# Seven block products for the gate chunks of the conv branch in a two-layer streaming encoder

## The chip, the cores and the metric

One core of a Trainium2 chip runs the whole program as one launch. The metric is the device time of the run in microseconds. A core has a matrix engine (TensorE, PE in the profile), VectorE (DVE), ScalarE (ACT), GpSimd (POOL) and SyncE (SP), each with a queue of its own that runs in order, and semaphores between them.

## What is computed

The reference is one step of a two-layer encoder on 544 token columns (512 of a prompt and 32 of a running stream) with 1024 channels. In each layer three branches, each 512 wide, are merged by sigmoid gates:

```python
gates = jax.nn.sigmoid(g.reshape(bsz, t_len, N_BRANCH, D_MODEL) + b_gate)
merged = (gates[:, :, 0] * (y_a @ w_branch[0])
          + gates[:, :, 1] * (y_b @ w_branch[1])
          + gates[:, :, 2] * (y_c @ w_branch[2]))
x = layer_norm(DN_ALPHA * x + merged @ w_out, ln1_g, ln1_b)
```

`g` is a slice of `x @ w_in`, so each branch's gate is a 1024 by 1024 matrix on the token columns. `y_a` comes from a width-31 convolution followed by a layer norm and SiLU, `y_b` from a gated mixing over 128 rows, `y_c` from stick-breaking attention. A ConvGLU channel mixer (w_up, a width-3 convolution, w_down) follows.

## The kernel before

**Numbers in two parts.** Every float32 operand of a matmul is split into a rounded high part (fp32r) and the rest: ScalarE writes the high part by a copy, VectorE the low part by a subtraction. A product is then three matmuls of 128 by 128 weights on 272 columns, high·high, high·low, low·high (`three_of`, lines 2053 to 2061).

**Tiles.** The 544 columns are two halves of 272 (`HALF`). Weights come in chunks: 2048 columns hold 8 contraction tiles of 256 outputs. A chunk gives four *units*, two output tiles times two halves, each in a PSUM bank `ps[0..3]` (named `acc`); unit b has output tile b % 2 and half b // 2. A unit over 8 contraction tiles is 24 matmuls, over 4 tiles 12.

**The ring of weights.** SP loads chunks in a fixed order into three slots (`raw`, `wh`, `wl`; `SLOT`, line 67), and waits for a slot until TensorE's first matmul after the slot's last use. The fourth w_out chunk (`OUT_LAST`) has a slot of its own in space of the convolution. ScalarE's `hi()` (line 577) and VectorE's `lo()` (line 1186) split the chunks in the same order.

**The branches.** Each layer takes them in the order attention, mixing, convolution (n = 0, 1, 2), each as four pairs i = 0..3 of a gate chunk (4 units of 24 matmuls) and a branch chunk (4 units of 12). The third branch's pairs are lines 2372 to 2374 on TensorE. ScalarE's `gates` (line 854) turns the four gate banks into sigmoids in `tmp`; VectorE's `products` (line 1587) multiplies them with the branch banks and adds to `merged` (lines 1608, 1611); for n = 2 ScalarE copies `merged` to `mh` (line 882), VectorE writes `ml` (line 1597), and both feed w_out. The order of each queue is written out by hand: in pair 0 of the third branch VectorE runs `lo()`, `conv_lo` (8 instructions at line 1225, the low part `yal` of `y_a`), `lo()`, `products(0, 2)`; ScalarE runs `conv_write` (lines 891, 893), then `gates(0, 2)`, then the `mh` copies.

**Seven products elsewhere.** In the FFN, 19 of the 22 pairs of w_up chunks already multiply a 2 by 2 block matrix with seven products instead of eight (`products` on TensorE, line 2412; sums of weights on VectorE, lines 1846 to 1866; sums of tokens T1 to T4N, line 1791). There the sums of a quad are made one to two quads ahead.

**POOL** is little used: masks for attention and, per layer, the low part of one w_up chunk (line 561).

Of the kernel before, what the change touches and what calls it, by code (L numbers as in the profile page):

```python
# [5 lines left out]
F32 = mybir.dt.float32  # L6
F32R = mybir.dt.float32r
# [4 lines left out]
P = 128  # L12
# [131 lines left out]
def trunk(nc, adds, x_in, win, wbr, wout, wup, wdn, par_in, bc_in, sguw_in, kc_in, vc_in, gh_in, fh_in,  # L144
          y_out, k_out, v_out, glu_out, ffn_out, sgu_out):
    with ExitStack() as ctx:
        sems = {}

        def sem(name):
            sems[name] = ctx.enter_context(nc.semaphore(name))  # L150
            return sems[name]
# [41 lines left out]
        mv = sb("mv", [P, 5, 2])  # L193
        rs = sb("rs", [P, 2, 5])

        gex = sb("gex", [P, 2, GEX])
        C = top[0]
        cbuf = sb("cbuf", [P, 2, GEX - 2])
# [55 lines left out]
        sqc = [sb("sqc0", [P, CT, HALF], at=F + 90016), sb("sqc1", [P, CT, HALF], at=F + 71168)]  # L254

        cst = [st0[:, :], cbuf[:, 0, 0:HALF]]
        csd = [st1[:, :], cbuf[:, 0, HALF:2 * HALF]]
# [96 lines left out]
        back_hi = sem("back_hi")  # L354
        fst_made = sem("fst_made")
        s_ready = sem("s_ready")
        prod_full = sem("prod_full")
        snapped = sem("snapped")
        combined = sem("combined")
# [34 lines left out]

        def dve_at(l, what, q):
            return l * len(DVE_ORDER) + DVE_PLACE[what, q]

        def first_chunk(l):
            return l * LAYER + 45
# [8 lines left out]
        def _(sp):  # L408
# [29 lines left out]
            for l in range(DEPTH):  # L438
# [81 lines left out]
        def _(pool):  # L520
# [18 lines left out]
            for r in range(DEPTH):  # L539
                pool.wait_ge(late_full, c.take(late_full, 64))  # L540
                g.affine_select(out=wsgu[:, :, :], in_=wsgu[:, :, :], compare_op=ALU.is_ge, fill=0.0, base=0,
                                         pattern=[[0, CT], [1, P]], channel_multiplier=-1).then_inc(
                                             sgu_masked, c.up(sgu_masked))

                for n in range(STEPS):
                    w = (n % 4 + 1) * P
                    for b in range(2):
                        pool.wait_ge(sig_full[b], c.take(sig_full[b]))
                        for t, fill in ((keep[b][:, T - P:T], 1.0), (beta[n % 2][b][:, w - P:w], 0.0)):
                            g.affine_select(out=t, in_=t, compare_op=ALU.is_gt, fill=fill, base=0, pattern=[[-1, P]],  # L550
                                            channel_multiplier=1).then_inc(mask_full[b], c.up(mask_full[b]))
                for b in range(2):
                    c.skip(sig_full[b], 2)

                j = r * LAYER + POOL_LO
# [16 lines left out]
        def _(act):  # L572
# [161 lines left out]
            for l in range(DEPTH):  # L734
# [119 lines left out]
                def gates(i, n, after=None, first=None):  # L854
# [50 lines left out]
                for n in range(3):  # L905
                    for i in range(4):
# [3 lines left out]
                            act.wait_ge(sgu_stored, c.take(sgu_stored, 16))  # L910
                        if n == 1 and i == 3:
                            gates(i, n, first=lambda: [conv_root(h) for h in range(2)])
                        else:
                            gates(i, n, mixed_hi if (n, i) == (0, 3) else squares if (n, i) == (1, 2) else None)
# [38 lines left out]
                      ACT.Copy).then_inc(fst_made, 1)  # L953

                def conv_taps(i):
                    act.wait_ge(acc_free[3], c.seen(acc_free[3]))
                    act.wait_ge(gex_full, c.take(gex_full))
                    for m in range(2):
# [182 lines left out]
        def _(dve):  # L1141
# [269 lines left out]
            for l in range(DEPTH):  # L1411
# [169 lines left out]
                def gated_lo():  # L1581
                    for g_ in range(CT):
                        dve.wait_ge(yb_hi, c.take(yb_hi))
                        v.tensor_tensor(yb[1][:, g_, :], gv[:, g_, :], yb[0][:, g_, :].bitcast(F32),
                                                 ALU.subtract).then_inc(yb_full, c.up(yb_full))

                def products(i, n):

                    for b in range(4):
# [303 lines left out]
                def gated_values(q):  # L1893
# [3 lines left out]
                    if q + 1 < QUADS:  # L1897
# [136 lines left out]
        def _(pe):  # L2034
# [199 lines left out]
            for r in range(DEPTH):  # L2234
# [342 lines left out]
```

## Time and profile before

| | us |
|---|---|
| runs: 1743.92, 1744.11, 1744.28; median | 1744.11 |
| profiled execution, its own time | 1744.08 |
| its span, first to last instruction | 1742.3 |
| TensorE busy | 1729.0 |
| VectorE busy | 1347.0 |
| ScalarE busy | 856.4 |
| POOL busy | 101.2 |

The span is what the timeline shows; the 1.8 us around it belong to the run's time. A matmul's listed length is its way through the pipeline, and matmuls overlap: what one costs is the distance from start to start. The same holds, less strongly, for VectorE and ScalarE, whose next instruction may start shortly before the last one ends. The third branch of layer 0 lies at 373 to 445 us, that of layer 1 at 1234 to 1306 us.

### The profile page before, as it was taken

The page shows a single profiled execution, that of the slowest core. Times are in us where ns is not written, and L with a number is a line of the kernel's source. Part 1 is how long each engine was busy: PE and PEld are TensorE (multiplying, and loading weights), DVE is VectorE, ACT ScalarE, POOL GpSimd, SP SyncE. Part 2 cuts the span into 40 slices and gives each one's busy share as a digit, 9 for nine tenths or more (in the row PEclk, how much of TensorE's full clock was granted, in tenths as well). Part 3 has the DMA queues.
Part 4 walks back from the last instruction along what each step waited for, and adds up shares of the span by engine and source line. Part 5 has one row for each costly group of instructions (what it writes and reads, how often), then busy time and mean ns, then how long its engine had stood idle before and what let it go on. Part 6 is the DMA issues. An engine that isn't in the chain of part 4 may idle for free.

```text
span 1742.3 us, 32677 instructions
## 1 busy us (share of the span) xinstructions
PE 1729.0 (99%) x13778; PEld 1694.6 (97%) x13778; DVE 1347.0 (77%) x1927; ACT 856.4 (49%) x1400; POOL 101.2 (6%) x159
## 2 busy tenths in 40 slices
PE   9999999999999999999999999999999999999997
PEld 9998899999999999999999989999999999999997
DVE  5698778664689999876667887777557999998675
ACT  4246532263366655644452565333534656656443
POOL 0025100000010000000000350000001000000000
PEclk9999999999999999999999999999999999999999
DMA  5432122222223223355524221222232222223544
GB/s 177 152 121 74 37 92 81 73 86 97 77 72 120 98 97 100 107 181 177 168 98 155 94 74 62 75 85 90 81 98 97 74 98 97 97 100 132 177 164 135
DMA packets 36513, 185.99 MB, mean 107 GB/s; under 512 B 7376, under 2 KB 11728, under 8 KB 18192
## 3 DMA queue, kind: packets, MB, share of 16 engines
q1 hardware_dynamic: 34672, 176.28, 30.3%
q10 hardware_dynamic: 1696, 7.64, 1.3%
q8 instruction: 109, 1.79, 0.4%
q14 instruction: 36, 0.29, 0.1%
HBM read 176.75 MB, written 7.15 MB: 106 GB/s over the span
## 4 chain that ended last, share of the span: by engine, by line
PE 96%; DVE 3%; issue 1%; DMA 0%; ACT 0%; ACTq 0%; DVEq 0%
PE acc L2055 23%; PE acc L2061 22%; PE acc L2060 22%; PE score L2055 5%; PE score L2061 5%; PE score L2060 5%; PE small L2060 1%; PE small L2061 1%; PE small L2055 1%; PE score L2131 1%; PE turned L2060 1%; PE turned L2061 1%; PE turned L2055 1%; PE small L2182 1%; PE turned L2162 1%; DVE acc L1397 1%
## 5 line engine op out<-in xcount | busy, mean ns | idle before, releaser
L2055 PE MATMUL acc<-xh,wh 128*128 128x272 f32 x1880 | 551.2, 293 | 1.3 <-DVE xl L1147 1.2
L2061 PE MATMUL acc<-xh,wl 128*128 128x272 f32 x1880 | 541.7, 288 | 0.0
L2060 PE MATMUL acc<-xl,wh 128*128 128x272 f32 x1880 | 541.1, 288 | 0.0
L1193 DVE TENSOR_TENSOR wl<-raw,wh 128x2048 fp32r<-128x2048 f32 (+2 forms) x116 | 231.5, 1995 | 171.5 <-ACT wh L584 170.9
L2055 PEld LDWEIGHTS acc<-xh,wh 128*128 128x128 f32 x1880 | 354.1, 188 | 8.8 <-issue 5.0
L2060 PEld LDWEIGHTS acc<-xl,wh 128*128 128x128 f32 x1880 | 354.2, 188 | 0.1
L2061 PEld LDWEIGHTS acc<-xh,wl 128*128 128x128 f32 x1880 | 353.2, 188 | 0.0
L584 ACT ACTIVATE wh<-raw 128x2048 fp32r<-128x2048 f32 (+2 forms) x136 | 232.7, 1711 | 162.7 <-DMA raw<-wdn 115.0
L2055 PE MATMUL acc<-fhh,wh 128*128 128x272 f32 x704 | 204.2, 290 | 0.1
L2060 PE MATMUL acc<-fll,wh 128*128 128x272 f32 x704 | 202.5, 288 | 0.0
L2061 PE MATMUL acc<-fhh,wl 128*128 128x272 f32 x704 | 202.4, 288 | 0.0
L1397 DVE SCALAR_TENSOR_TENSOR acc<-glu,par,acc 128x574 f32<-128x574 f32 x240 | 181.1, 812 | 0.1
L862 ACT ACTIVATE tmp<-acc,par 128x272 f32<-128x272 f32 x96 | 46.6, 488 | 195.5 <-PE acc L2061 195.2
L2055 PEld LDWEIGHTS acc<-fhh,wh 128*128 128x128 f32 x704 | 132.6, 188 | 0.7 <-issue 0.5
L2060 PEld LDWEIGHTS acc<-fll,wh 128*128 128x128 f32 x704 | 132.4, 188 | 0.2
L2061 PEld LDWEIGHTS acc<-fhh,wl 128*128 128x128 f32 x704 | 132.4, 188 | 0.0
L2055 PE MATMUL score<-th,shi 128*128 128x272 f32 x304 | 88.4, 291 | 0.0
L2061 PE MATMUL score<-th,slo 128*128 128x272 f32 x304 | 87.8, 289 | 0.0
L2060 PE MATMUL score<-tl,shi 128*128 128x272 f32 x304 | 87.1, 287 | 0.0
L2055 PE MATMUL acc<-mh,wh 128*128 128x272 f32 x256 | 74.9, 293 | 0.0
L2060 PE MATMUL acc<-ml,wh 128*128 128x272 f32 x256 | 73.8, 288 | 0.0
L2061 PE MATMUL acc<-mh,wl 128*128 128x272 f32 x256 | 73.7, 288 | 0.0
(325 smaller groups left out, 3939.5 us busy)
## 6 DMA issues: line engine op xcount, KB each, us to landing
raw<-win SPq DMA_DIRECT2D x50, 1024.0 KB, 5.0
raw<-wup SPq DMA_DIRECT2D x44, 1024.0 KB, 5.0
raw<-wdn SPq DMA_DIRECT2D x32, 1024.0 KB, 4.9
raw<-wbr SPq DMA_DIRECT2D x24, 512.0 KB, 3.6
raw<-wdn SPq DMA_DIRECT2D x16, 768.0 KB, 4.2
raw<-wout SPq DMA_DIRECT2D x8, 1024.0 KB, 4.9
v_out<-vfm ACTq DMA_DIRECT2D x2, 1088.0 KB, 9.2
k_out<-k ACTq DMA_DIRECT2D x2, 1088.0 KB, 4.9
```

What stands on the lines that cost most here:

```text
L584: A(wh[s][:, 0:n], raw[s][:, 0:n], ACT.Copy).then_inc(hi_full[s], c.up(hi_full[s]))
L862: A(tmp[:, b, :], ps[b][:, 0:HALF], ACT.Sigmoid, bias=col(par, PAR["b_gate"] + 8 * BRANCHES[n] + 2 * i + b % 2)).then_inc(acc_free[b], c.u ...
L1193: v.tensor_tensor(wl[s][:, 0:n], raw[s][:, 0:n], wh[s][:, 0:n].bitcast(F32), ALU.subtract).then_inc(lo_full[s], c.up(lo_full[s]))
L1397: v.scalar_tensor_tensor(out=acc[:, m, :], in0=glu_at(m, j), scalar=w, in1=acc[:, m, :], op0=ALU.mult, op1=ALU.add).then_inc(vec, c.up(vec))
L2055: first = mm(out, a, xs[0], start=start, stop=False, skip_group_check=onto)
L2060: mm(out, a, xs[1], start=False, stop=False, skip_group_check=onto)
L2061: return mm(out, b, xs[0], start=False, stop=stop, skip_group_check=onto)
L2131: last = mm(bs[b][:, 0:w], yc[x][rows, ht, i * P:w], ks[y][rows, ht, 0:w], start=x + y == 0, stop=y == 1)
L2162: last = pe.transpose(bt[:, kb * P:(kb + 1) * P], beta[n % 2][part][:, kb * P:(kb + 1) * P], ident[:, :])
L2182: last = mm(bo[DH * b:DH * b + DH, kb * P:SEQ], vtok[:, kb, h * DH:(h + 1) * DH], blocks.rearrange("p a n -> p (a n)"), start=kb == 0, sto ...
```

## The change

In the third branch, the gate chunks of pairs 1 to 3 are computed as block products with seven multiplications; pair 0 stays as it was. The chunk's 2 by 2 blocks are A11, A12 (contraction tiles 0 to 3 and 4 to 7 of output tile 0) and A21, A22 (of output tile 1). The tokens are halved in the same way. Each product is 4 tiles times 3 matmuls = 12 matmuls, 84 in all against 96:

| | product | bank |
|---|---|---|
| 1 | A11 · x(0..3, half 0) | GA = `bs[0]`, then snapshot m1 |
| 2 | A12 · x(4..7, half 0) | GB = `bo` |
| 3 | (A21 + A22 − A11) · T2 | on top of GA, then snapshot u1 |
| 4 | (A11 − A21) · T3 | GC = `bs[1]` |
| 5 | (A21 + A22) · T1 | on top of GA, then snapshot u3 |
| 6 | (A12 − (A21 + A22 − A11)) · x(4..7, half 1) | on top of GA |
| 7 | A22 · T4N | on top of GC |

The gates are: unit 0 from GB + m1, unit 3 from GC + u3 (before product 7), unit 2 from GA after product 6, unit 1 from GC + u1 after product 7. TensorE runs products 1 to 5, branch unit 0, product 6, branch unit 1, product 7, branch units 2 and 3.

- **POOL** makes the four token sums T1, T3, T2, T4N once per layer, 1088 columns each, in buffers of the convolution, after the variance matmuls of the convolution's layer norm.
- **ScalarE** splits them in pair 0, between its gates, after waiting for the end of `conv_lo`; it also splits the weights and weight sums and takes the snapshots.
- **VectorE** makes the weight sums (four of 512 columns per pair), their low parts, the low parts of the token sums, and the three additions of snapshots per pair. In pair 0 these preparations of pair 1 stand ahead of `products(0, 2)`.
- **SP** waits for product 5 of pair 3 before it loads the fourth w_out chunk, whose slot lies in the same buffers.
- The squares of the convolution's norm (`sqc`) move to other space; two columns of `gex` are zeroed again by VectorE.

The diff, cut to what orders the work:

```diff
@@ sync
                     if i == 3:
                         sp.wait_ge(ya_full, c.take(ya_full, 2 * CT))
+                        sp.wait_ge(gprod_full, 7 * gquad(l, 3) + 5)
@@ gpsimd
+                pool.wait_ge(glu_stored, 16 * 2 * CT * (r + 1))
+                pool.wait_ge(ln_var, 2 * (r + 1))
...
+                    if n > 1:
+                        pool.wait_ge(gt_made, 4 * r + (1 if n == 2 else 3))
+                    g.tensor_tensor(gtraw[j][:, :, :], a, b, ALU.subtract).then_inc(gt_made, 1)
@@ scalar, gates(i, n)
-                        if n == 2 and b == 2:
-                            hi()
+                def gate_turned_hi(j):
+                    act.wait_ge(gt_made, 4 * (l + 1))
+                    act.wait_ge(ya_full, 2 * CT * (l + 1))
+                    A(gth[j][:, :, :], gtraw[j][:, :, :], ACT.Copy).then_inc(gt_hi, 1)
+                def make_ready(b):
+                    if b == 0:
+                        gate_turned_hi(T2)
+                        gate_turned_hi(T3)
+                    if b == 1:
+                        gate_turned_hi(T1)
+                        gate_turned_hi(T4N)
+                    if b == 2:
+                        gate_first_blocks(1)
+                        gate_second_blocks(1)
+                    if b == 3:
+                        gate_two_sums(1)
+                        gate_last_sum(1)
+                def block_gates(i):
+                    gate_snapshot("m1", i, 1)
+                    hi()
+                    gate_snapshot("u1", i, 3)
+                    gate_sigmoid(i, 0, 1)
+                    gate_snapshot("u3", i, 5)
+                    gate_sigmoid(i, 3, 2)
+                    if i == 3:
+                        hi()
+                    gate_first_blocks(i + 1)
+                    gate_two_sums(i + 1)
+                    gate_sigmoid(i, 2)
+                    gate_last_sum(i + 1)
+                    gate_second_blocks(i + 1)
+                    gate_sigmoid(i, 1, 3)
...
+                        elif n == 2 and i:
+                            block_gates(i)
@@ vector, block_products(i)
+                    gate_add(i, 0, GB, "m1", 2, 1)
+                    lo()
+                    gate_add(i, 3, GC, "u3", 5, 3)
+                    gate_three_sums(i + 1)
+                    if i == 3:
+                        lo()
+                    one(0)
+                    gate_fourth_sum(i + 1)
+                    gate_first_low(i + 1)
+                    gate_two_lows(i + 1)
+                    gate_add(i, 1, GC, "u1", 7, 2)
+                    one(1)
+                    if i == 3:
+                        low(0)
+                        low(1)
+                    gate_back_low(i + 1)
+                    one(2)
+                    one(3)
...
                 for h in range(2):
                     conv_lo(h)
-                lo()
+                gate_turned_lo(T2)
+                gate_turned_lo(T3)
+                gate_three_sums(1)
+                gate_fourth_sum(1)
+                gate_turned_lo(T1)
+                gate_first_low(1)
+                gate_back_low(1)
+                gate_two_lows(1)
+                gate_last_low(1)
                 products(0, 2)
-                for i in range(3):
-                    lo()
-                    lo()
-                    products(i + 1, 2)
+                gate_turned_lo(T4N)
+                for i in range(1, 4):
+                    block_products(i)
...
+                v.memset(gex[:, :, 0:2], 0.0).then_inc(gex_zeroed, 1)
                 history(0)
@@ tensor
-                for i in range(4):
-                    chunk()
-                    chunk(xs=ya, nk=CT, first=ya_tiles if i == 0 else None)
+                chunk()
+                chunk(xs=ya, nk=CT, first=ya_tiles)
...
+                    if p == 2:
+                        pe.wait_ge(lo_full[s], c.take(lo_full[s]))
+                    if i > 1 and p in (1, 2, 4):
+                        pe.wait_ge(*{1: (gate_made, 4 * q - 1), 2: (gcombined, 3 * q - 2), 4: (gcombined, 3 * q)}[p])
+                    if p in (3, 5, 6):
+                        pe.wait_ge(gsnapped, 3 * q + {3: 1, 5: 2, 6: 3}[p])
+                    if p in (3, 6):
+                        pe.wait_ge(gs_ready, 2 * q + {3: 1, 6: 2}[p])
+                    if p == 7:
+                        pe.wait_ge(gcombined, 3 * q + 2)
+                    turned = {3: T2, 4: T3, 5: T1, 7: T4N}.get(p)
+                    if i == 1 and turned is not None:
+                        pe.wait_ge(gt_ready, 4 * r + G_ORDER[turned])
...
+                for i in range(1, 4):
+                    s = arrived()
+                    for p in range(1, 6):
+                        gate_product(i, p, s)
+                    sb_ = arrived()
+                    unit(sb_, 0, 0, ya, CT)
+                    gate_product(i, 6, s)
+                    unit(sb_, 1, 1, ya, CT)
+                    gate_product(i, 7, s)
+                    unit(sb_, 2, 0, ya, CT)
+                    unit(sb_, 3, 1, ya, CT, done=True)
```

`gate_snapshot` copies bank GA to an SBUF buffer; `gate_sigmoid` waits for its addition or product and writes `tmp`; `gate_add` adds a bank and a snapshot; `one(b)` is the two product instructions of unit b, `low(b)` the `ml` instruction. The four `mh` copies of a pair stay in ScalarE's `products(i, 2)`, which runs after `gates` or `block_gates` of that pair and before those of the next.

## Rows read from the trace of the kernel before

**Rows 1.** the page, part 1: busy us (share of the span), instructions

```profile
PE 1729.0 (99%) x13778; PEld 1694.6 (97%) x13778; DVE 1347.0 (77%) x1927; ACT 856.4 (49%) x1400; POOL 101.2 (6%) x159
```

**Rows 2.** TensorE's waits, whole run: waited for, us in total, times, longest

```profile
PE acc L2055 <- DVE xl L1147: 1.2, 1, 1.2
```

**Rows 3.** TensorE's timeline: start us, us, instruction; first matmuls of three stages

```profile
385.16 0.29 PE L2055 MATMUL acc<-yah,wh 128*128 128x272 f32 x1
...
391.20 0.29 PE L2055 MATMUL acc<-xh,wh 128*128 128x272 f32 x1
...
403.23 0.29 PE L2055 MATMUL acc<-yah,wh 128*128 128x272 f32 x1
```

**Rows 4.** busy time by window: us, then PE, PEld, DVE, ACT, POOL

```profile
391.00:409.00 18.00, 18.00 (x145) 18.00 (x145) 8.44 (x15) 6.43 (x10) 0.00 (x0) 1.00 0.28 88
```

**Rows 5.** ScalarE's timeline, 350 to 420 us

```profile
354.80 0.49 ACT L594 ACTIVATE st<-small,eps 128x272 f32<-128x272 f32 x1 [0.31 <-PE small L2110]
...
381.37 1.48 ACT L862 ACTIVATE tmp<-acc,par 128x272 f32<-128x272 f32 x3
```

**Rows 6.** POOL's timeline, 1340 to 1355 us

```profile
1345.54 5.63 POOL L561 TENSOR_TENSOR wl<-raw,wh 128x512 fp32r<-128x512 f32 x4 [296.62 <-ACT wh L584]
```

**Rows 7.** VectorE's timeline, 350 to 420 us and 1346 us

```profile
368.86 0.44 DVE L1608 TENSOR_TENSOR tmp<-acc,tmp 128x272 f32<-128x272 f32 x1 [5.93 <-PE acc L2061]
...
369.70 2.28 DVE L1193 TENSOR_TENSOR wl<-raw,wh 128x2048 fp32r<-128x2048 f32 x1
...
381.23 2.90 DVE L1225 TENSOR_TENSOR yal<-acc,yah 128x272 fp32r<-128x272 f32 x8
...
386.93 0.44 DVE L1608 TENSOR_TENSOR tmp<-acc,tmp 128x272 f32<-128x272 f32 x1
...
388.44 0.44 DVE L1608 TENSOR_TENSOR tmp<-acc,tmp 128x272 f32<-128x272 f32 x1 [0.59 <-PE acc L2061]
...
391.47 0.44 DVE L1608 TENSOR_TENSOR tmp<-acc,tmp 128x272 f32<-128x272 f32 x1 [0.35 <-PE acc L2061]
...
392.31 1.02 DVE L1597 TENSOR_TENSOR ml<-merged,mh 128x272 fp32r<-128x272 f32 x2
...
1346.09 1.42 DVE L1234 TENSOR_TENSOR st<-cbuf 128x272 f32<-128x272 f32 x1
```

**Rows 8.** ScalarE's groups, shapes apart: busy us, mean ns of one | idle before

```profile
L981 ACT ACTIVATE wh<-raw 128x1024 fp32r<-128x1024 f32 x38 | 40.4, 1062 | 59.0 <-DVE raw L1852 59.0
...
L1002 ACT ACTIVATE m<-score 128x272 f32<-128x272 f32 x38 | 15.0, 395 | 11.5 <-PE score L2061 10.9
...
L882 ACT ACTIVATE mh<-merged 128x272 fp32r<-128x272 f32 x32 | 13.8, 431 | 42.3 <-DVE merged L1611 42.3
...
L968 ACT ACTIVATE th<-traw 128x1088 fp32r<-128x1088 f32 x8 | 8.9, 1112 | 3.7 <-DVE traw L1791 3.6
```

**Rows 9.** VectorE's groups, shapes apart, the same columns

```profile
L1816 DVE TENSOR_TENSOR wl<-raw,wh 128x1024 fp32r<-128x1024 f32 x38 | 46.3, 1218 | 0.0
...
L1846 DVE TENSOR_TENSOR sraw<-raw 128x512 f32<-128x512 f32 x38 | 26.0, 684 | 1.2 <-DMA raw<-wup 1.2
...
L1797 DVE TENSOR_TENSOR tl<-traw,th 128x1088 fp32r<-128x1088 f32 x8 | 10.1, 1286 | 0.1
```

**Rows 10.** VectorE's timeline in the FFN, 559 to 562 us

```profile
559.23 1.22 DVE L1808 TENSOR_TENSOR wl<-raw,wh 128x1024 fp32r<-128x1024 f32 x1
560.36 1.22 DVE L1816 TENSOR_TENSOR wl<-raw,wh 128x1024 fp32r<-128x1024 f32 x1
```

**Rows 11.** timelines of VectorE and ScalarE, 446 to 455 us

```profile
448.92 2.29 DVE L1193 TENSOR_TENSOR wl<-raw,wh 128x2048 fp32r<-128x2048 f32 x1 [1.37 <-ACT wh L584]
...
450.55 1.92 ACT L584 ACTIVATE wh<-raw 128x2048 fp32r<-128x2048 f32 x1 [1.67 <-DMA raw<-wout]
```

**Rows 12.** busy time and granted clock by window at the end: columns as above, PEclk after POOL

```profile
1731.00:1734.00 3.00, 0.93 (x4) 0.42 (x3) 2.54 (x4) 1.21 (x3) 2.50 (x3) 1.00 0.00 0
1734.00:1737.00 3.00, 0.00 (x0) 0.00 (x0) 2.93 (x4) 0.93 (x2) 1.43 (x2) 0.56 0.00 0
```

More of the change, by code:

```diff
@@ L356, in trunk @@
         s_ready = sem("s_ready")
+        gt_made = sem("gt_made")
+        gt_hi = sem("gt_hi")
+        gt_ready = sem("gt_ready")
+        gs_made = sem("gs_made")
+        gs_hi = sem("gs_hi")
+        gs_ready = sem("gs_ready")
+        gback_hi = sem("gback_hi")
+        gprod_full = sem("gprod_full")
+        gsnapped = sem("gsnapped")
+        gcombined = sem("gcombined")
+        gate_made = sem("gate_made")
+        gex_zeroed = sem("gex_zeroed")
         prod_full = sem("prod_full")
@@ new lines, in gate_fourth_sum, with gate_first_low @@
+                def gate_fourth_sum(i):
+                    if i < 4:
+                        a11, a12, a21, a22 = gate_blocks(i)
+                        q = gquad(l, i)
+                        dve.wait_ge(gs_made, 4 * q + 3)
+                        if i > 1:
+                            dve.wait_ge(gprod_full, 7 * (q - 1) + 6)
+                        v.tensor_tensor(gate_sum(2), a12, gate_sum(1), ALU.subtract).then_inc(gs_made, 1)
+                def gate_first_low(i):
+                    if i < 4:
+                        s, n = SLOT[turn[0]], CHUNK // 2
+                        assert turn[0] == gate_chunk(l, i)
+                        turn[0] += 1
+                        dve.wait_ge(hi_full[s], c.take(hi_full[s]))
+                        dve.wait_ge(gs_made, 4 * gquad(l, i) + 3)
+                        v.tensor_tensor(wl[s][:, 0:n], raw[s][:, 0:n], wh[s][:, 0:n].bitcast(F32), ALU.subtract).then_inc(
+                            lo_full[s], c.up(lo_full[s]))
@@ new lines, in gate_last_low, with gate_add @@
+                def gate_last_low(i):
+                    if i < 4:
+                        dve.wait_ge(gs_hi, 2 * gquad(l, i) + 2)
+                        v.tensor_tensor(gslo4[:, :], gsraw4[:, :], gshi4[:, :].bitcast(F32), ALU.subtract).then_inc(
+                            gs_ready, 1)
+                def gate_add(i, b, bank, name, product, snapshot):
+                    dve.wait_ge(gprod_full, 7 * gquad(l, i) + product)
+                    dve.wait_ge(gsnapped, 3 * gquad(l, i) + snapshot)
+                    dve.wait_ge(m_sum, c.seen(m_sum) if b != 1 else c.seen(m_sum, 1))
+                    v.tensor_tensor(tmp[:, b, :], bank[:, 0:HALF], snap[0][name][:, :], ALU.add).then_inc(gcombined, 1)
@@ new lines, in block_products, with one, low @@
+                def block_products(i):
+                    def one(b):
+                        t, cols = 2 * i + b % 2, (b // 2 * HALF, (b // 2 + 1) * HALF)
+                        dve.wait_ge(gate_made, 4 * gquad(l, i) + (1, 4, 3, 2)[b])
+                        dve.wait_ge(acc_full[b], c.take(acc_full[b]))
+                        v.tensor_tensor(tmp[:, b, :], ps[b][:, 0:HALF], tmp[:, b, :], ALU.mult).then_inc(
+                            acc_free[b], c.up(acc_free[b]))
+                        dve.wait_ge(acc_free[b], c.seen(acc_free[b]))
+                        v.tensor_tensor(row(merged, t, *cols), row(merged, t, *cols), tmp[:, b, :], ALU.add).then_inc(
+                            m_sum, c.up(m_sum))
+                    def low(b):
+                        t, cols = 2 * i + b % 2, (b // 2 * HALF, (b // 2 + 1) * HALF)
+                        dve.wait_ge(m_hi, c.take(m_hi))
+                        v.tensor_tensor(row(ml, t, *cols), row(merged, t, *cols), row(mh, t, *cols).bitcast(F32),
+                                        ALU.subtract).then_inc(m_ready[b // 2], c.up(m_ready[b // 2]))
+                    gate_add(i, 0, GB, "m1", 2, 1)
[16 more added lines that the diff above has]
+                    one(3)
+                    if i < 3:
+                        low(0)
+                        low(1)
+                    gate_last_low(i + 1)
+                    low(2)
+                    low(3)
@@ L2371, in ya_tiles, with gate_product @@
                         pe.wait_ge(ya_full, c.take(ya_full))
-                for i in range(4):
-                    chunk()
-                    chunk(xs=ya, nk=CT, first=ya_tiles if i == 0 else None)
+                chunk()
+                chunk(xs=ya, nk=CT, first=ya_tiles)
+                pe.wait_ge(mixed_used, c.seen(mixed_used))
+                def gate_product(i, p, s):
+                    q = gquad(r, i)
+                    if p == 2:
[11 more added lines that the diff above has]
+                        pe.wait_ge(gt_ready, 4 * r + G_ORDER[turned])
+                    bank = {2: GB, 4: GC, 7: GC}.get(p, GA)
+                    for t in range(4):
+                        if p in (1, 2, 4, 7):
+                            at = {1: t * 256, 2: (4 + t) * 256, 4: t * 256 + P, 7: (4 + t) * 256 + P}[p]
+                            w = [x[s][:, at:at + P] for x in (wh, wl)]
+                        elif p == 6:
+                            w = [x[:, t * P:(t + 1) * P] for x in (gshi4, gslo4)]
+                        else:
+                            w = [x[:, {5: 0, 3: 1}[p], t * P:(t + 1) * P] for x in (gshi, gslo)]
+                        if turned is None:
+                            tile, h = {1: (t, 0), 2: (4 + t, 0), 6: (4 + t, 1)}[p]
+                            mv_ = [x[:, tile, dcol(h)] for x in xs]
+                        else:
+                            mv_ = [x[turned][:, t, :] for x in (gth, gtl)]
+                        last = three_of(bank[:, 0:HALF], w, mv_, p in (1, 2, 4) and t == 0, t == 3, p not in (1, 2, 4))
+                    last.then_inc(gprod_full, 1)
+                    if p == 7:
+                        read.append(s)
```

93 lines of the change are left out of this document (91 added, 2 removed).

## The prediction, on record before the kernel ran

> **What bounds the kernel now.** I read the page's busy shares first. TensorE is busy for 99% of the span, VectorE for 77%, ScalarE for 49% [rows 1]. Next I read TensorE's waits over the whole run: the longest single one is 1.2 us, at the very start [rows 2]. So every matmul that goes away saves its own time, and every wait put on TensorE's queue costs its full length; nothing later can take up either. The price of a matmul comes from TensorE's timeline in the third branch: the branch half of pair 0 starts at 385.16, that of pair 1 at 403.23, one pair of 144 matmuls apart, so 18.07/144 = 0.1255 us each, and a unit of 12 costs 1.51 us [rows 3]. The listed 0.29 us of a matmul is its length in the pipeline, not its price. Last I looked at what the other two engines have to do in one such pair: VectorE 8.44 us, ScalarE 6.43 us of 18 [rows 4]. They look idle, but they run strictly in order, and their order is what the change rewrites. I therefore worked along their queues.
>
> All times below are those of layer 0. Layer 1 has the same program, so per-layer figures are doubled.
>
> **What goes away.** Each of three pairs per layer needs 84 gate matmuls in place of 96: 36 per layer, 72 in all, 72 × 0.1255 = 9.04 us [rows 3].
>
> **POOL's four sums.** They wait for the variance matmuls, whose result ScalarE reads at 354.80 [rows 5]. POOL's 512-column subtractions took 5.63 us for four, 2.75 ns a column, so 1088 columns cost 3.0 us and four sums 12 us: done by about 367 [rows 6]. The first reader is ScalarE after 381.85 [rows 5]. Behind POOL's new wait stands only its later split of one w_up chunk. VectorE can suffer: a 272-column addition of two SBUF operands took 1.42 us beside POOL, where 272-column instructions otherwise take 0.44 [rows 6, 7]. The bounds are no delay, and 12 us of VectorE held, of which 5.93 us is its idle time before 368.86 [rows 7]. The remaining 6.1 us would move the split of gate chunk 0 from 369.70 to 375.8, its end to 378, and TensorE, which is due to start on it at 373.1, would be 5 us late. I book nothing for it, since that loss would fall inside the larger wait worked out next, which begins from ScalarE's work and not from TensorE's. The Trainium skill, "SBUF — State Buffer", says of the engine ports that VectorE and GpSimd take their shared pair as an exclusive lock for a whole instruction when a VectorE instruction has two SBUF inputs. By that rule the four 3.0 us sums would hold VectorE one after another, which is the upper bound above; the 1.42 us row agrees, and the sum stays the same.
>
> **The first block pair (the term that decides).** ScalarE's split of the token sum T2 waits until VectorE has finished all of `yal`, at 381.23 + 2.90 = 384.13 [rows 7]. Queued behind that wait on ScalarE stand three of pair 0's four gates and all preparations of pair 1. With 1.11 us for T2 [rows 8], VectorE may start T2's low part at 385.30. From there its queue holds, before the products of pair 0: three 1088-column lows, four 512-column sums, three 1024-column lows, one 512-column low. Their durations are 1.29, 0.68 and 1.22 us [rows 9]; back to back an instruction starts 0.09 before its forerunner ends (559.23 + 1.22 against 560.36) [rows 10]. Two sums wait for the one before, 0.12 each. So 3 × 1.20 + 4 × 0.60 + 0.24 + 3 × 1.13 + 0.60 = 10.2 us, and the first product starts at 395.5. (ScalarE's twelve pieces in the same stretch come to some 9 us, so it does not set this.) In the trace of before, the products of pair 0 stand at 386.93, and their second pair of lows starts at 392.31, 5.38 us later, with 0.59 and 0.35 us of waiting for TensorE in it: 4.44 us of work [rows 7]. The last sum is then ready at about 400.0. ScalarE still has to copy it to `mh` (0.43) and only then, in its order, comes snapshot m1 of pair 1 (0.40) [rows 8]: 400.9 with hand-overs.
>
> TensorE's side: pair 1 starts at 391.20 if nothing waits, and product 3 of it, two units later, at 394.21 [rows 3]. Product 3 writes into the bank that m1 is read from, and waits for the snapshot. **So 400.9 − 394.2 = 6.7 us per layer are lost there.** About 1.9 us of it shows earlier, since the gates of units 2 and 3 of pair 0, pushed behind the token splits, hold their banks until 389.1 (384.16, four splits of 1.02, gate 1, gate 2) and 391.6 (two 1024-column splits of 0.97 and gate 3 more), where the branch units want them at 388.2 and, after that delay, 390.7 [rows 3, 5, 8]; the other 4.6 to 4.8 us is one wait at product 3. The bounds: 5.5 us if hand-overs are free and ScalarE gets in earlier, 8 us if issue gaps come in.
>
> **The pairs after it.** From the end of product 7 the chain is: addition, gate 1, two product instructions, a 1024-column low, four more product instructions, `mh`, m1. With the durations above that is 5.9 to 6.1 us, against four units = 6.03 us until product 3 of the next pair. I take 0.15 us for each of two hand-overs, 0.3 per layer (bounds 0 and 0.8). The work itself fits: VectorE gains about 5 us per pair (three additions, four sums, one and a half lows), 13.7 of 16.6; ScalarE about 2.4.
>
> **The second w_out chunk.** Its ring slot was freed six units before the stage's end. Now it is freed after product 7, two units before it (−3.0). The third chunk shows the latency: slot free at 391.20 + 3 × 18.07 = 445.4, split begun at 450.55 when the transfer let go [rows 11]. So +5.1, then 1.92 and 2.29 for the two splits [rows 11]: ready at +6.4 against +6.0, where TensorE has used up the first chunk. Before, it was ready at 451.2 against 451.4. I take 0.4 us per layer (bounds 0 and 1).
>
> **At no cost.** SP's new wait before the fourth w_out chunk is over nine units before that chunk's turn, hidden by the third chunk's wait for its slot; uncovered, it would hold the w_up loads behind it. The two zeroed columns of `gex` are one small VectorE instruction ahead of a much longer ScalarE chain; if that cover went it would be some 0.2 us.
>
> **The sum.** Profiled execution 1744.08 (its span of 1742.3 and 1.8 around it; the median of the runs is 1744.11, so nothing to convert). 1744.08 − 9.04 + 2 × (6.7 + 0.3 + 0.4) = **1749.8 us**. The change takes 9 us of matmuls away and gives 14.8 back as waits, nearly all of it where the stage goes over to the block products.
>
> **Rivals.**
> *A. TensorE alone decides (faster).* If the snapshot m1 of pair 1 came before 394.2, with pair 1's preparations fitting beside pair 0, only the w_out wait stays: 1744.08 − 9.04 + 0.8 = 1735.8 us. It speaks for it that TensorE waits nowhere now, also not in the FFN's quads, which use the same seven-product order [rows 2]. Against it: those quads are prepared one to two quads ahead, and here the queue orders put pair 0's products behind 10.2 us of preparation. The point from which it decides: m1 ready 4 us earlier than I work out, when the loss equals the gain. Chance 0.12.
> *B. The wait is there, but 1.2 to 4 us shorter per layer* (less of VectorE's list ahead of the products than I count): 1749.8 less 2.4 to 8, so 1742 to 1747.4 us. Chance 0.18.
> *C. The wait also drops TensorE's clock.* In the last stage the granted clock is 0.56 in 1734 to 1737, with no matmul in it, after 1.00 before [rows 12]: an idle of 3 to 6 us took it from the 2.4 to the 1.2 GHz level. The wait here is 4.6 us. No row shows how it comes back; if it stays low for as long as the engine had idled, each wait costs a further 2.3 us, 1749.8 + 4.6 = 1754.4. It may fall in one layer and not in the other. Chance 0.15. The Trainium skill, "TensorE: Matmul & The Clock Gate", section "HAM oscillation", says that a wait between groups of matmuls throttles the clock again and the next group starts cold; that is this rival, and row 12 agrees with the falling half of it.
> *D. The forecast*, 1747 to 1752. Chance 0.55.
> That the change does less than it says is excluded by counting: 13778 matmuls must become 13706 [rows 1].
>
> **How the numbers follow.** The likeliest case is D, at 1749.8; its own range by the bounds is 1744.08 − 9.04 + 11 = 1746.0 to 1744.08 − 9.04 + 19.6 = 1754.6. The range to quote takes in most of B below, 1743, and C above, 1755; A and the fringe of B are left out. A measurement of this kernel can tell about 0.2%, 3.5 us, from no change: faster is below 1740.6, slower above 1747.6. Faster is A, 0.12. B, with the lower fringe of D, is the same: 0.18 + 0.03 = 0.21. Slower is C and the rest of D: 0.67.
>
> **What would show it.** In the changed profile: 13706 matmuls; in TensorE's waits one of 4 to 5 us in each layer at a product into a `score` bank, released by a ScalarE snapshot that came after the fourth `mh` copy; two of about 0.9 us before units of pair 0's branch half, released by gates; a few tenths at the second w_out chunk; none elsewhere over 0.5 us. VectorE busy from 385 to 400 without a gap. I am wrong if ScalarE's first snapshot stands well before the last `mh` copies of pair 0, or if that wait is under 2 us; if VectorE stands still under POOL from 355 on, with TensorE idle near 373, the loss sits earlier than I put it, but the sum should hold.

## The result, and the profile after

The changed kernel takes 1756.59 us (median of 6 runs, 1755.99 to 1757.14), the kernel before 1744.19 us in the same comparison (6 runs, 1743.92 to 1745.58): ratio 1.0069, 95% interval 1.0059 to 1.0079. It is slower by 12.4 us. I had forecast 1749.8 us, 5.7 us slower, and a range up to 1755. The direction and the place were right; the size was not, and the result lies outside the range. The profiled execution took 1756.83 us, with a span of 1755.1.

First the page's part 1, the answer to [rows 1]:

```profile
PE 1727.7 (98%) x13706; PEld 1690.2 (96%) x13706; DVE 1397.5 (80%) x1997; ACT 878.7 (50%) x1444; POOL 126.2 (7%) x167
```

The 72 matmuls are gone (13778 to 13706), yet TensorE's busy time fell by only 1.3 us, where 72 × 0.1255 = 9.04 us should have gone. So some of the remaining matmuls must run longer, besides the new idle time. TensorE's waits over the whole run (columns as in [rows 2]) show the idle part:

```profile
PE score L2296 <- ACT m L960: 8.6, 2, 4.3
PE acc L2296 <- ACT tmp L909: 2.8, 4, 0.8
PE acc L2296 <- DVE xl L1268: 2.7, 2, 1.6
PE acc L2296 <- DVE wl L1314: 1.1, 2, 0.5
```

The first line is product 3 of pair 1 waiting for snapshot m1, once per layer. The second is the branch units of pair 0 waiting for its late gates. The third is the start of the run, before any of the change. The last is the second w_out chunk. Why m1 is late is read from ScalarE's timeline in layer 0:

```profile
384.63 2.12 ACT L942 ACTIVATE gth<-gtraw 128x1088 fp32r<-128x1088 f32 x2 [2.37 <-DVE yal L1346]
386.65 0.47 ACT L909 ACTIVATE tmp<-acc,par 128x272 f32<-128x272 f32 x1
...
389.02 0.47 ACT L909 ACTIVATE tmp<-acc,par 128x272 f32<-128x272 f32 x1
...
391.61 0.47 ACT L909 ACTIVATE tmp<-acc,par 128x272 f32<-128x272 f32 x1
...
397.00 0.43 ACT L999 ACTIVATE mh<-merged 128x272 fp32r<-128x272 f32 x1 [3.46 <-DVE merged L1844]
...
400.43 0.43 ACT L999 ACTIVATE mh<-merged 128x272 fp32r<-128x272 f32 x1 [0.40 <-DVE merged L1844]
400.77 0.38 ACT L960 ACTIVATE m<-score 128x272 f32<-128x272 f32 x1
```

ScalarE waits 2.37 us for `yal`, splits the token sums, and so makes gates 2 and 3 late. Then it idles 3.46 us until the first `mh` copy may start, and m1 follows only the fourth. VectorE's timeline gives the reason:

```profile
385.78 2.50 DVE L1710 TENSOR_TENSOR gtl<-gtraw,gth 128x1088 fp32r<-128x1088 f32 x2 [1.24 <-ACT gth L942]
...
396.06 0.44 DVE L1841 TENSOR_TENSOR tmp<-acc,tmp 128x272 f32<-128x272 f32 x1
...
399.95 0.44 DVE L1844 TENSOR_TENSOR merged<-merged,tmp 128x272 f32<-128x272 f32 x1
```

From 385.78 to 396.06 it prepares pair 1, without a gap; only then come the products of pair 0, the last sum at 399.95. What TensorE does meanwhile stands in its own timeline:

```profile
396.63 0.29 PE L2302 MATMUL small<-xh,wl 128*128 128x272 f32 x1
401.20 0.60 PE L2296 MATMUL score<-gth,gshi 128*128 128x272 f32 x1 [4.28 <-ACT m L960]
401.59 0.43 PE L2301 MATMUL score<-gtl,gshi 128*128 128x272 f32 x1
401.82 0.43 PE L2302 MATMUL score<-gth,gslo 128*128 128x272 f32 x1
```

Start to start the stall is 401.20 − 396.63 − 0.1255 = 4.44 us. Behind it the matmuls start 0.227 us apart instead of 0.1255, and one lasts 0.43 us instead of 0.29. Windows of the same stretch (window, its length, then busy us and instructions of PE, PEld, DVE, ACT, POOL; PEclk, the granted clock as a share of full speed; DMA share; GB/s):

```profile
391.00:397.00 6.00, 5.12 (x39) 4.69 (x37) 5.97 (x8) 2.54 (x4) 0.00 (x0) 1.00 0.33 93
397.00:401.20 4.20, 0.00 (x1) 0.00 (x1) 3.80 (x10) 2.06 (x6) 0.00 (x0) 0.87 0.28 117
401.20:404.00 2.80, 2.80 (x12) 2.80 (x13) 2.80 (x4) 0.89 (x1) 0.00 (x0) 0.50 0.00 0
404.00:407.00 3.00, 3.00 (x16) 3.00 (x15) 0.02 (x1) 0.81 (x2) 0.00 (x0) 0.52 0.00 0
407.00:410.00 3.00, 3.00 (x27) 3.00 (x26) 0.95 (x2) 0.87 (x2) 0.00 (x0) 1.00 0.00 0
```

The granted clock falls in the stall and stands at 0.50, the 1.2 GHz level, until about 407: 12 and 16 matmuls in windows that hold 22 and 24 at full speed. From 401.20 to 406.80 there are 24 starts; at full speed they take 3.01 us, here 5.60, a loss of 2.59 us. This shows as busy time, not as a wait. Layer 1 repeats it (0.50 from 1268 to 1271, 0.52 to 1274).

Two ScalarE table loads enclose the stage, first before, then after:

```profile
380.07 1.28 ACT L862 ACT_TABLE_LOAD   x1
474.01 1.28 ACT L614 ACT_TABLE_LOAD   x1
```

```profile
380.48 1.28 ACT L909 ACT_TABLE_LOAD   x1
480.57 1.28 ACT L661 ACT_TABLE_LOAD   x1
```

The stage takes 93.94 us before and 100.09 after. So layer 0 lost 6.15 us net, and layer 1, read the same way, 6.22. With the 4.52 us of matmuls saved, that is 10.7 us given away per layer: 0.77 and 0.95 at pair 0's units, 4.44 at product 3, 2.59 of half clock, 0.14 to 0.23 at each of pairs 2 and 3, 0.68 to 0.69 at the second w_out chunk. The remaining 0.9 or so is in gaps that I did not separate. About 0.4 us came in ahead of the stage: the wait at the start of the run is 1.72 us from start to start, where it was 1.31.

### The profile page after: what moved, and what is told of

Read it like the earlier page. It is cut to its first block, busy times and chain, and to the rows that moved or that the text cites. A ratio compares the mean times of both kernels' runs of the same rounds, so it can differ in the third digit from the quotient of the medians.

```text
span 1755.1 us, 32736 instructions
## 1 busy us (share of the span) xinstructions
PE 1727.7 (98%) x13706; PEld 1690.2 (96%) x13706; DVE 1397.5 (80%) x1997; ACT 878.7 (50%) x1444; POOL 126.2 (7%) x167
## 4 chain that ended last, share of the span: by engine, by line
PE 89%; DVE 6%; ACT 3%; issue 2%; DMA 0%; ACTq 0%; DVEq 0%
PE acc L2296 20%; PE acc L2302 19%; PE acc L2301 19%; PE score L2296 6%; PE score L2302 6%; PE score L2301 6%; PE small L2301 1%; PE small L2302 1%; PE small L2296 1%; PE score L2372 1%; PE turned L2301 1%; PE turned L2302 1%; PE turned L2296 1%; PE turned L2403 1%; PE small L2423 1%
## 5 line engine op out<-in xcount | busy, mean ns | idle before, releaser
L2296 PE MATMUL acc<-xh,wh 128*128 128x272 f32 x1688 | 495.8, 294 | 2.9 <-DVE xl L1268 2.7
L2302 PE MATMUL acc<-xh,wl 128*128 128x272 f32 x1688 | 486.4, 288 | 0.0
L2301 PE MATMUL acc<-xl,wh 128*128 128x272 f32 x1688 | 485.8, 288 | 0.0
L2296 PEld LDWEIGHTS acc<-xh,wh 128*128 128x128 f32 x1688 | 317.9, 188 | 10.6 <-issue 6.3
L2301 PEld LDWEIGHTS acc<-xl,wh 128*128 128x128 f32 x1688 | 318.0, 188 | 0.1
L1314 DVE TENSOR_TENSOR wl<-raw,wh 128x2048 fp32r<-128x2048 f32 (+2 forms) x110 | 217.6, 1979 | 125.8 <-ACT wh L631 125.1
L2302 PEld LDWEIGHTS acc<-xh,wl 128*128 128x128 f32 x1688 | 317.1, 188 | 0.0
L2302 PE MATMUL score<-xh,wl 128*128 128x272 f32 x272 | 78.7, 289 | 0.0
L2296 PE MATMUL score<-xh,wh 128*128 128x272 f32 x272 | 78.7, 289 | 0.0
L2301 PE MATMUL score<-xl,wh 128*128 128x272 f32 x272 | 78.2, 288 | 0.0
```

Source lines behind the costliest of these rows:

```text
L1314: v.tensor_tensor(wl[s][:, 0:n], raw[s][:, 0:n], wh[s][:, 0:n].bitcast(F32), ALU.subtract).then_inc(lo_full[s], c.up(lo_full[s]))
L2296: first = mm(out, a, xs[0], start=start, stop=False, skip_group_check=onto)
L2301: mm(out, a, xs[1], start=False, stop=False, skip_group_check=onto)
L2302: return mm(out, b, xs[0], start=False, stop=stop, skip_group_check=onto)
```

## The experiments

My theory: ScalarE's and VectorE's queue order in pair 1 makes the stall, and the stall costs twice, by its length and by the half clock behind it. Rivals: the slow matmuls belong to the new operands and banks; the seven-product order costs this by itself; POOL's sums take part of it.

**e1_filler.** Keep TensorE at work in the wait:

```
+                    if p == 3 and i == 1:
+                        for _ in range(32):
+                            mm(bt[:, 0:HALF], wh[s][:, 0:P], xs[0][:, 0, dcol(0)], start=True, stop=True)
                     if p in (3, 5, 6):
                         pe.wait_ge(gsnapped, 3 * q + {3: 1, 5: 2, 6: 3}[p])
```

> The changed kernel with 32 further matmuls of 272 columns, of operands that are on hand, into an idle PSUM bank, issued by TensorE in branch pair 1 right before the product that waits for the snapshot m1 (in the changed kernel that wait is 4.4 us at 400 us and again in layer 1, and the matmuls behind it stand 0.23 us apart for 5.6 us). Extra work that no output uses. Theory (the wait costs twice: its own length, and about 2.4 us per layer of half clock behind it): the fillers take 32 x 0.1255 = 4.0 us of the 4.4 us wait, so the product goes at the same moment, the matmuls behind it stand 0.125 us apart with the clock shown as 1.0, and the time falls by about 4.8 us to 1751.8 us. Rival (the slow matmuls belong to the operands or the bank they use, not to the idle time before them): still 0.23 us apart, 1756.6 us or above.

Measured: 1751.72 us (5 runs, 1751.40 to 1753.43), ratio to before 1.0043 (1.0029 to 1.0057). 64 more matmuls make the changed kernel 4.9 us faster, 2.43 per layer. Its windows:

```profile
397.00:401.20 4.20, 3.94 (x32) 3.71 (x31) 3.80 (x11) 2.07 (x6) 0.00 (x0) 1.00 0.26 109
401.20:404.00 2.80, 2.80 (x23) 2.80 (x24) 2.70 (x4) 1.58 (x3) 0.00 (x0) 1.00 0.00 0
404.00:407.00 3.00, 3.00 (x26) 3.00 (x26) 0.58 (x2) 0.51 (x2) 0.00 (x0) 1.00 0.00 0
```

The fillers fill the wait, product 3 starts at 401.08, where it started at 401.20, and the same matmuls, on the same operands and banks, run at full clock. The rival of operands and banks falls.

**e2_m1_first.** Only ScalarE's order: m1 ahead of pair 0's `mh` copies.

```
                 def block_gates(i):
                     gate_snapshot("m1", i, 1)
+                    if i == 1:
+                        products(0, 2)
                     hi()
...
-                        products(i, n)
+                        if (n, i) != (2, 0):
+                            products(i, n)
```

> The changed kernel with only ScalarE's order altered: in pair 1 the snapshot m1 is taken ahead of the four mh copies of pair 0, which now follow it. Theory (ScalarE's queue behind VectorE's late products of pair 0 is what holds m1, and the other snapshots stand behind it in the same queue): the 4.4 us wait at product 3 goes, a wait of about 2.5 us comes up at product 5 (for u1, behind the mh copies) and one of 0.4 us at the first unit of the next branch; with a shorter stall TensorE's clock may hold: 1746 to 1747 us if it does, about 1751 us if it falls as before. Rival (only m1's place matters): no wait takes its place, 4.4 + 2.4 us per layer come back, 1743 us or less.

Measured: 1749.08 us (7 runs, 1748.79 to 1750.50), ratio 1.0027 (1.0016 to 1.0038). The wait moved as expected, to product 5 and snapshot u1:

```profile
PE score L2299 <- ACT u L960: 4.4, 2, 2.2
```

Start to start it is 2.34 us, and 0.31 at the next branch; in the profiled execution the clock kept 1.00 in both layers. From the changed kernel 2 × (4.44 + 2.59 − 2.34 − 0.31) = 8.8 us should have come back, and 7.5 did; I had put 1746 to 1747 us for a clock that holds. In the profiled execution (1748.79) the two stages did give it back: between their table loads they are 4.48 and 4.44 us shorter than in the changed kernel. But 0.89 us came in between the two stages, outside the changed code (767.80 us where the changed kernel has 766.91). In two of the other executions (1749.73, 1750.50) the mean clock is lower, 0.996 against 0.998; whether it fell behind the stall there is not shown. The order of the queue is the cause, and m1's place is not all of it.

**e3_reorder.** The order of the first block pair changed on both engines (the core of it):

```
                 def make_ready(b):
                     if b == 0:
+                        gate_first_blocks(1)
+                        gate_second_blocks(1)
+                        gate_two_sums(1)
+                    if b == 1:
                         gate_turned_hi(T2)
                         gate_turned_hi(T3)
...
                     gate_snapshot("u1", i, 3)
+                    if i == 1:
+                        products(0, 2)
...
+                gate_three_sums(1)
+                gate_fourth_sum(1)
                 lo()
                 for h in range(2):
                     conv_lo(h)
...
+                products(0, 2, lambda: gate_turned_lo(T1))
```

> The changed kernel with the first block pair's preparation moved: the weight sums of pair 1 before the lo parts of branch chunk 0 on VectorE (which idles there between 375 and 380 us), weight splits before token splits, and pair 0's mh copies on ScalarE after pair 1's last snapshot u1, its ml subtractions on VectorE after the lo parts of branch chunk 1. Pairs 2 and 3 as in the changed kernel. Theory (all but about 1.5 us per layer of the loss is the first pair's queue order and the clock it drops): no wait of TensorE at pair 1 over 1 us, clock 1.0 throughout, 9.04 us of matmuls saved less some 1.5 us per layer: about 1738.2 us. Rival (the seven-product order with its snapshots costs this by itself, wherever the preparation stands): waits come back at the other snapshots, 1744 us or more.

Measured: 1740.28 us (9 runs, 1738.84 to 1743.25), ratio 0.9978 (0.9968 to 0.9988): 16.3 us faster than the changed kernel, with the same 13706 matmuls. ScalarE's timeline:

```profile
392.93 0.40 ACT L960 ACTIVATE m<-score 128x272 f32<-128x272 f32 x1 [2.25 <-PE score L2303]
...
396.24 1.38 ACT L1001 ACTIVATE mh<-merged 128x272 fp32r<-128x272 f32 x4
```

The snapshot now waits for TensorE and not the other way round, and the four `mh` copies run in one go behind u1. The clock is 1.00 in every window from 373 to 445. The median is 2 us above my sum. In the profiled execution (1740.40) the stages, between their table loads, are 2.40 and 2.46 us shorter than before, so 2.1 us of the 4.52 saved per layer are lost, not 1.5; another 1.0 us came in between the stages. Of TensorE's waits on ScalarE only this is left:

```profile
PE score L2297 <- ACT m L960: 1.0, 2, 0.5
```

**e4_reorder_all.** The same order for pairs 2 and 3:

```
                     gate_snapshot("u1", i, 3)
+                    products(i - 1, 2)
...
                     gate_add(i, 0, GB, "m1", 2, 1)
                     lo()
+                    for b in range(4):
+                        low(b, i - 1)
```

> As the kernel with the first pair's preparation moved, and the same order for pairs 2 and 3: the mh copies of the pair before after the snapshot u1, the ml subtractions after the lo parts of the next branch chunk. Theory: the two waits of 0.25 to 0.8 us at product 3 of pairs 2 and 3 go as well, and only the wait of the second output-weight chunk (0.6 to 0.8 us per layer) is left: about 1736.4 us. Rival (those hand-overs are paid for wherever the copies stand, or the moved copies delay the output weights more): 1738 us or more, no faster than the kernel that moves the first pair alone.

Measured: 1738.51 us (5 runs, 1737.01 to 1739.47), ratio 0.9963 (0.9951 to 0.9976). The m1 waits are gone from the list. The median is 1.8 us under that of e3_reorder, just the step expected, but 2 us above my figure and within the rival's 1738 us or more, and the ranges of the two overlap by 0.6 us. The traces settle it: between their table loads the stages are 1.18 and 1.14 us shorter than in e3_reorder, so the rival (no faster) falls.

**e5_wout.** In addition the weight copy of the second w_out chunk before the last two `mh` copies, its lo part before the last two `ml`:

```
+                            if (i, b) == (3, 1):
+                                hi()
...
-                    for r in range(3):
+                    for r in range(2):
                         hi()
...
                     if i == 3:
+                        lo()
                         low(2)
                         low(3)
```

> The kernel with the preparation moved for all pairs, and one more step: the weight copy of the second output-weight chunk on ScalarE right after the second of pair 3's four mh copies (before: after the fourth), and its lo part on VectorE ahead of the last two ml subtractions. Theory (that chunk's weights come late only because they stand behind mh copies that its first units do not need): the wait of 0.69 us per layer at the second output-weight chunk goes, 1.4 us in all, about 1737.1 us against 1738.5 us. Rival (something else, as the chunk's transfer, holds it): the wait stays, 1738.5 us.

Measured: 1737.21 us (5 runs, 1736.53 to 1738.29), ratio 0.9957 (0.9944 to 0.9969), the lowest median of the study. Half right: the wait fell from 0.69 to 0.41 us in layer 0 and to 0.37 in layer 1, and did not go. ScalarE, and TensorE's wait:

```profile
443.27 1.92 ACT L631 ACTIVATE wh<-raw 128x2048 fp32r<-128x2048 f32 x1 [2.22 <-DMA raw<-wout]
```

```profile
PE acc L2295 <- DVE wl L1318: 0.5, 2, 0.3
```

With the copies out of the way the chunk's transfer ends last: SP issues it at 438.42, after the first matmul behind product 7 (438.10), and ScalarE waits for it until 443.27. So 0.28 us was queue, and 0.41 is the slot that is freed later. Between their table loads the stages are 0.21 and 0.17 us shorter than in e4_reorder_all. The medians differ by 1.3 us, but the ranges overlap; no more than the 0.4 us is shown.

**e6_sums.** The kernel before plus POOL's sums alone:

```
+                pool.wait_ge(glu_stored, 16 * 2 * CT * (r + 1))
+                pool.wait_ge(ln_var, 2 * (r + 1))
...
+                    g.tensor_tensor(gt[n % 4][:, :, :], a, b, ALU.subtract).then_inc(gt_made, 1)
```

> The kernel before with one part of the change alone: GpSimd's four token sums per layer at their place (and the moved buffers of the normalised convolution that they need); nothing uses the sums, all products are made as before. Theory (GpSimd holds VectorE's four normalisation products of the convolution for about 2.8 us a pair of them, and VectorE was going to idle for 5.9 us right behind them): VectorE's rows as in the changed kernel (4.2 us where 1.4 us stood), the idle time behind them gone, and no change of the time: 1744.1 us, within 0.5 us. Rival (the sums cost part of the 12.4 us by which the changed kernel is slower): 1746 us or more.

Measured: 1743.87 us (11 runs, 1743.59 to 1745.55), ratio 0.9999 (0.9990 to 1.0008). VectorE's timeline, first one line of before, then this run:

```profile
358.41 1.36 DVE L1219 TENSOR_TENSOR sqc<-acc,st 128x544 f32<-128x544 f32 x2
```

```profile
358.46 4.16 DVE L1233 TENSOR_TENSOR sqc<-acc,st 128x544 f32<-128x544 f32 x2
362.54 1.84 DVE L1229 RECIPROCAL cbuf<-cbuf 128x272 f32<-128x272 f32 x1
364.41 4.18 DVE L1233 TENSOR_TENSOR sqc<-acc,cbuf 128x544 f32<-128x544 f32 x2
368.92 0.44 DVE L1622 TENSOR_TENSOR tmp<-acc,tmp 128x272 f32<-128x272 f32 x1 [0.33 <-PE acc L2076]
```

Each pair of products takes 4.2 us where it took 1.36 in the trace of before; the reciprocal between them keeps its 1.84 us (1.85 before), though POOL is at work. The 5.93 us of idle time in [rows 7] are used up to 0.33, and the time does not move.

**e7_sums_twice.** The same with each sum made twice:

```
-                                            (x_at[1][1], gt[0][:, :, :]), (x_at[1][0], gt[2][:, :, :]))):
+                                            (x_at[1][1], gt[0][:, :, :]), (x_at[1][0], gt[2][:, :, :])) * 2):
```

> As the kernel before with the token sums alone, but each sum made twice, so that GpSimd works from 356 to about 381 us. Theory (VectorE is held by GpSimd for as long as both are at work, and the cover ends at 368.9 us): VectorE's additions and its lo part of branch chunk 0, between 369 and 374 us, are held as well, TensorE waits for them, 1 to 6 us per layer slower: 1746 to 1756 us. Rival (VectorE's longer rows before were a matter of those four instructions, not of GpSimd's work): no change, 1744.1 us.

Measured: ratio 1.0038 (1.0024 to 1.0051), four runs of 1749.12 to 1753.90 us; a fifth took 4332 us and is left out. VectorE is held beyond the cover, and the list of TensorE's waits has one new line:

```profile
369.32 1.91 DVE L1625 TENSOR_TENSOR merged<-merged,tmp 128x272 f32<-128x272 f32 x1
371.16 4.63 DVE L1207 TENSOR_TENSOR wl<-raw,wh 128x2048 fp32r<-128x2048 f32 x1
375.71 0.43 DVE L1622 TENSOR_TENSOR tmp<-acc,tmp 128x272 f32<-128x272 f32 x1
```

```profile
PE acc L2070 <- DVE wl L1207: 5.1, 2, 2.6
```

Start to start it is 2.72 us per layer, and two of them are 5.4: the faster executions (1749.12, 1749.55) are before plus just that. In the profiled one (1753.90) the clock fell to 0.50 behind the stall in both layers; here layer 0:

```profile
376.00:379.00 3.00, 3.00 (x14) 3.00 (x15) 2.93 (x4) 3.00 (x7) 2.92 (x2) 0.50 0.47 123
```

**e8_stall.** The kernel before, without any block product, and a stall made by POOL:

```
+                pool.wait_ge(acc_full[0], (33, 82)[r])
+                for n in range(4):
+                    g.tensor_tensor(gt[0][:, n, :], xT[:, n, 0:HALF], xT[:, n, 0:HALF], ALU.subtract).then_inc(stalled, 1)
...
+                        pe.wait_ge(stalled, 4 * (r + 1))
...
-                    chunk()
+                    chunk(end=stall if i == 1 else None)
```

> The kernel before, with no block product in it, and a stall of TensorE alone: after the first unit of gate chunk 1 of the third branch TensorE waits until GpSimd, released by that unit, has made four subtractions of 272 columns that nothing uses (about 4.2 us; VectorE has nothing to do in that time). Theory (the half clock follows an idle TensorE, whatever the kernel computes): behind the stall the matmuls stand 0.23 us apart with the clock shown as 0.5 for some 5.6 us, 2.4 us per layer, on top of the stall: 1744.1 + 2 x (4.2 + 2.4) = about 1757.3 us. Rival (the half clock belongs to the seven-product order, its operands or banks): the stall alone, about 1752.5 us, the matmuls behind it 0.125 us apart.

Measured: 1754.61 us (5 runs, 1752.02 to 1757.68), ratio 1.0058 (1.0045 to 1.0070). TensorE's waits and the windows of layer 0:

```profile
PE acc L2063 <- POOL gt L561: 6.1, 2, 3.0
```

```profile
397.00:399.00 2.00, 0.00 (x0) 0.00 (x0) 0.01 (x1) 0.00 (x0) 2.00 (x4) 0.85 0.28 115
399.00:401.00 2.00, 1.64 (x7) 1.65 (x8) 0.00 (x0) 0.00 (x0) 0.30 (x1) 0.50 0.00 0
401.00:404.00 3.00, 3.00 (x15) 3.00 (x14) 0.00 (x0) 0.00 (x0) 0.00 (x0) 0.50 0.00 0
404.00:407.00 3.00, 3.00 (x22) 3.00 (x21) 0.00 (x0) 0.49 (x1) 0.00 (x0) 0.80 0.00 0
```

POOL was quicker than I took it for: the stall is 3.18 us start to start. The half clock follows it, in a kernel that has no block product. By the enclosing table loads (382.03 and 481.89) the layer is 5.92 us longer, so 2.7 us stand behind the stall. The median, too, is 4.3 us above the kernel before with the two stalls added (1743.98 + 6.36 = 1750.3). The executions spread over 5.7 us, and the longer the time, the lower the mean clock (0.997 at 1752.02, 0.993 at 1757.68). The profiled one is the longest; in the others less of the stretch behind the stall can have run at the low level.

## Why the prediction was right and wrong

**The matmuls saved: right.** 72 fewer; and with most of the waits gone the stages of e5_wout are 3.79 and 3.77 us shorter than before, of the 4.52 saved per layer. About half of the rest is the wait at the second w_out chunk.

**POOL's sums: booked at nothing, which came out right, but not for my reason.** The upper bound, all 12 us of VectorE held, did not come: the convolution's four products were held, 2 × 2.8 = 5.6 us in all, and the reciprocal between them was not (e6_sums). The idle time of 5.93 us took that up with 0.33 us to spare, which is luck, since I had not worked out the 5.6. My reason, that such a loss would fall inside the larger wait, was tested by no run. The cover ends there: twice the sums cost 2.72 us per layer (e7_sums_twice).

**The first block pair: right in cause and size.** I had the first product on VectorE at 395.5 and m1 done at 400.9; they came at 396.06 and 401.15. The 6.7 us became 0.77 + 0.95 + 4.44 = 6.2. That the order alone does it is shown by e2_m1_first (the wait moves one snapshot on) and e3_reorder (it goes). One figure of rival A was off: by my own terms the loss equals the gain when m1 is ready 2.9 us earlier, 6.7 + 0.3 + 0.4 − 4.52, not 4.

**The pairs after it: right.** 0.15 us a hand-over forecast, 0.14 to 0.23 measured.

**The second w_out chunk: 0.4 forecast, 0.69 measured.** The 0.4 of the late slot is there, 0.41 in e5_wout. The 0.28 above it is the copy's place behind pair 3's `mh` copies, which I did not count, though I had counted just that for m1.

**The step that failed: rival C.** I gave "the wait also drops TensorE's clock" a chance of 0.15 and left it out of the sum. It happened in both layers, at 2.59 us each against the 2.3 I had priced. With it and the measured w_out term my own sum is 1744.08 − 9.04 + 2 × (6.7 + 0.3 + 0.69 + 2.59) = 1755.6 us, 1 us from the result. The evidence lay on the table: [rows 12] showed an idle TensorE losing its clock (with 0.93 us of work in the first of the two windows, after 2 to 5 us, not the 3 to 6 that I read), the forecast itself held a stall of 4.6 us, and no row showed such a stall with the clock kept. For a chance as low as 0.15 I gave no reason, though that row was the only observation. That the 2.3 came near the 2.59 is in part luck: I had priced a low clock for as long as the stall, and it lasted 5.60 us behind 4.44, and from 399.4 to beyond 404 behind the 3.18 of e8_stall. The range failed with it: its upper end took C with all other terms at their middle values.

The Trainium skill, "TensorE: Matmul & The Clock Gate", section "HAM oscillation", says that a wait between groups of matmuls throttles the clock again and that the next group starts cold. The changed kernel and e8_stall agree (0.50 behind waits of 4.44 and 3.18 us); behind the 2.34 us of e2_m1_first's profiled execution the clock stayed at 1.00.

**Is the change a bad one?** No: its order is. The same arithmetic with the preparation moved (e5_wout) is faster than before, ratio 0.9957.

## What to carry to other kernels

When work is moved onto engines that look half idle, follow their queues instruction by instruction, and look above all for a release (a snapshot, a copy) that stands behind another stage's waits in the same queue. Price a stall of several microseconds (3.2 and 4.4 here) on a TensorE that is otherwise always busy at its length plus the half clock behind it, and look for that second part in the granted clock and the spacing of the matmuls, since no list of waits shows it. Where the stall can't be moved, matmuls of no use in it can pay: 32 of them in each stall gave back 2.4 us of it here.

## What the runs showed of the hardware beyond that

- The clock comes back by itself while TensorE works: behind 4.44 us of stall it stood at 0.50 for about 5.6 us, behind 3.18 us in e8_stall until between 404 and 407, behind the 2.72 us of e7_sums_twice's profiled execution until about 379, 3 us. A shorter stall does not always bring it down: with 2.72 us (e7_sums_twice) executions that match the stall alone, 1749.1 and 1749.5 us, stand beside one of 1753.9 us whose clock fell in both layers. What decides it there these runs do not show.
- POOL's subtractions held VectorE's instructions with two SBUF inputs (a 272-column addition took 1.9 to 2.3 us instead of 0.44), but not those that read PSUM: `tmp<-acc,tmp` at 375.71 took its usual 0.43 us with POOL at work (e7_sums_twice). POOL pays too: its second round of the last two sums took 7.28 us where the first took 6.01.
